# S5 entry and exit and second MLP entry of a hybrid trunk kernel: splits, scalings and sums at other places of the engines' programs

## Chip, cores and metric

The kernel runs on one core of a Trainium2 chip. The metric is the device time of one launch in microseconds; lower is better. Engines are named as in the profile: PE is TensorE, DVE is VectorE, ACT is ScalarE, POOL is GpSimd, and SP is the sequencer that issues most of the DMAs.

## What is computed

The input is 256 frames of 2048 channels in float32, and there are two layers. Layer 0 is an RG-LRU beside sliding-window attention, followed by an MLP. Layer 1, which the change touches, is cut to this:

```
h = rmsnorm(x, mix_norm_o)
y = s5_grouped(h, ...)          # 128 groups: 16 channels in, 64 complex states, scan over frames, 16 out
g = gelu(y) @ w_glu             # 2048 x 4096
val, gate = split(g)
x = x + val * sigmoid(gate)
h = rmsnorm(x, ffn_norm[1])
x = x + square(relu(h @ w_up)) @ w_down      # 2048 x 8192 x 2048
```

## The kernel before, in words

The engines run programs of their own, in order, tied by semaphores. Nearly all of the time is matrix products on TensorE in float32r. Every product is made of a high and a low part of both operands, so a weight goes through three steps. SP loads a unit of 512 KB into one of four buffers `raw`. ScalarE makes the high part `Wh` (line 1162), and VectorE the difference `Wl` (line 1575). SP loads a buffer again only when VectorE has split it. `split(g, s)` is unit s of pair g; four units make a pair. ScalarE's `split` waits for the unit's landing and until TensorE is done with the unit that was in the buffer before.

The norm of the S5 layer: TensorE sums squares (line 1025), ScalarE takes the root, VectorE inverts it and signals `rss_ready` (line 1619, in `inv_root`). The root scales the S5 inputs `us`.

The S5 stage works on 16 chunks c of 128 channels each:

- `s5_input(c)` (line 2402, GpSimd) multiplies the chunk by the inverse root. Six chunks are done ahead of the loop, the others beside it, as `inputs_beside` lists. `input_rows` (line 2382) issues the DMA that brings two chunks of `us` in another order.
- `s5_in(c)` (line 1000, TensorE) multiplies by the input weights. From c = 13 (`V_ALONE`) on it has one result bank instead of two.
- `s5_rotate(c)` (lines 2009 and 2010, VectorE) multiplies by cosine and sine; `s5_turned(c)` (line 2409, GpSimd) takes their difference; `s5_scan(c)` (line 2018 and two multiplications, lines 2023 and 2024, VectorE) runs the recurrence and turns back; `s5_unturned(c)` (line 2415, GpSimd) sums.
- `s5_out(c)` (lines 1013 and 1018, TensorE) multiplies by the output weights; `s5_gelu(c)` (line 1443, ScalarE) follows and signals `s5_ge`.
- SP stores the result (line 619) and loads it in the order of frames, `load_turned` (line 608). It does the latter for chunk c only after the low part of chunk c - 4 is done.
- `s5_high(c)` (line 1448, ScalarE) and `s5_low(c)` (line 2421, GpSimd) make the operand of the GLU and signal `a2_ready`. GpSimd does the low parts of chunks 0 to 7 inside its loop, and those of 8 to 15 after `s5_unturned(15)`.

The order within each engine is written out by hand. SP's program ahead of and in the S5 loop is this; `load_glu` (line 601) loads a GLU unit:

```
for u in range(2 * NU): load_glu(0, u)          # NU = 4
...
for c in range(KC):
    sp.wait_ge(s5_ge, c + 1)                    # then the store of chunk c
    ...                                         # parameter rows of later chunks
    if c >= 1: load_turned(c - 1)
load_turned(KC - 1)
for u in range(2 * NU, 4 * NU): load_glu(0, u)
```

The GLU goes in four blocks j of 16 units. A unit of block 0 has two halves (frames 0 to 127 and 128 to 255) of six products each. From chunk 8 on TensorE does one half (`glu_piece`) per step of the S5 loop, in the order of `GLU_PIECES`, and the remaining units after the last output (`glu_block(0, 4)`, lines 1046 to 1048). Each block ends with a gate, a sum into `xin`, and a transposition back to channels (`turn_back`).

The second MLP's first pair of units needs the operands of GLU block 3 in its last unit: TensorE turns them back beside the second unit, and ScalarE (`operand_back`, line 1501) and VectorE (line 1934) make high and low parts. For the norm ScalarE squares the frames (`frame_squares(3)`, line 1492), VectorE makes two diagonals (line 1949), TensorE sums (`frame_sum`, line 1121, after the first pair), ScalarE loads the root's table and takes the root (lines 1185 and 1187), and VectorE inverts it (`rms`) before it reads the first pair's result.

## Time and profile before

| | us |
|---|---|
| runs shown | 2005.13, 2011.80, 2007.59 |
| their median | 2007.59 |
| the profiled execution: its time | 2006.38 |
| the profiled execution: its span | 2004.6 |

The span is from the first to the last instruction in the profile, 1.8 us less than the execution's own time. In the span TensorE is busy for 1967.2 us, VectorE for 1294.2, ScalarE for 927.6 and GpSimd for 705.8. The S5 stage lies at about 1048 to 1125 us, the GLU from there to about 1290, and the second MLP behind it. A matmul's end is modelled in the profile, and successive ones overlap, so start-to-start distances are the ones to read.

### The profile page before, as it was taken

The numbers are of one execution on the slowest core, as the hardware profiler recorded it, in microseconds if no ns is written. First come the engines' busy times: TensorE is split into PE (matmuls) and PEld (weight loads), VectorE is DVE, ScalarE is ACT, GpSimd is POOL, SyncE is SP. The second block draws the span as 40 slices with busy tenths as digits, with TensorE's granted clock in tenths as the row PEclk, the third lists the DMA queues.
The fourth block names the chain that finished last, engine by engine and source line by source line (L and its number), as shares of the span: only waits on it lengthen the run. The fifth ranks groups of instructions, "written<-read, shape, count | busy, mean of one in ns | idle before, by whom it ended". The sixth has DMA issues, their size and how long they took to land.

```text
span 2004.6 us, 32978 instructions
## 1 busy us (share of the span) xinstructions
PE 1967.2 (98%) x12214; PEld 1682.6 (84%) x12214; DVE 1294.2 (65%) x1428; ACT 927.6 (46%) x1211; POOL 705.8 (35%) x893
## 2 busy tenths in 40 slices
PE   8999999999999999999998999999999999999999
PEld 7778888888888888888887788888888888888887
DVE  6886787765765676567669555576556556655654
ACT  6456654444444444444553544544344434434442
POOL 3483368998777778440239300000000000000000
PEclk9999999999999999999998999999999999999999
DMA  7544568666766676676888566655566566555654
GB/s 224 172 123 130 169 180 225 192 210 214 225 201 221 197 224 205 218 250 204 275 272 298 181 185 179 188 182 192 194 187 191 190 192 186 189 194 184 189 193 164
DMA packets 326549, 400.29 MB, mean 200 GB/s; under 512 B 23328, under 2 KB 267184, under 8 KB 324368
## 3 DMA queue, kind: packets, MB, share of 16 engines
q1 hardware_dynamic: 318992, 371.77, 58.9%
q0 software_dynamic: 5216, 24.52, 4.0%
q8 instruction: 98, 1.61, 0.3%
q10 hardware_dynamic: 2208, 2.11, 0.3%
q14 instruction: 35, 0.29, 0.0%
HBM read 371.87 MB, written 25.17 MB: 198 GB/s over the span
## 4 chain that ended last, share of the span: by engine, by line
PE 89%; DVE 5%; ACT 2%; POOL 2%; issue 1%; DMA 1%; SPq 0%; ACTq 0%; POOLq 0%; DVEq 0%
PE ps L724 38%; PE ps L725 19%; PE ps L691 6%; PE ps L692 6%; PE ps L693 6%; DVE Wl L1575 2%; PE px L1047 1%; PE px L1048 1%; PE px L1046 1%; PE ps L1046 1%; PE ps L1047 1%; PE ps L1048 1%; PE px L944 1%; ACT Wh L1162 1%; POOL us L2402 1%
## 5 line engine op out<-in xcount | busy, mean ns | idle before, releaser
L724 PE MATMUL ps<-A,Wh 128*128 128x512 f32 x3520 | 1239.2, 397 | 4.5 <-issue 2.1
L1575 DVE TENSOR_TENSOR Wl<-raw,Wh 128x1024 fp32r<-128x1024 f32 x660 | 837.8, 1281 | 591.8 <-ACT Wh L1162 589.0
L1162 ACT ACTIVATE Wh<-raw 128x1024 fp32r<-128x1024 f32 x660 | 690.7, 1058 | 738.7 <-PE ps L725 446.5
L725 PE MATMUL ps<-A,Wl 128*128 128x256 f32 x3520 | 981.2, 279 | 0.0
L724 PEld LDWEIGHTS ps<-A,Wh 128*128 128x128 f32 x3520 | 661.1, 188 | 165.0 <-issue 6.9
L725 PEld LDWEIGHTS ps<-A,Wl 128*128 128x128 f32 x3520 | 663.3, 188 | 0.4
L691 PE MATMUL ps<-Wh,A 128*128 128x512 f32 x512 | 199.2, 389 | 0.0
L692 PE MATMUL ps<-Wl,A 128*128 128x512 f32 x512 | 199.2, 389 | 0.0
L693 PE MATMUL ps<-Wh,A 128*128 128x512 f32 x512 | 199.2, 389 | 0.0
L691 PEld LDWEIGHTS ps<-Wh,A 128*128 128x128 f32 x512 | 96.1, 188 | 20.1
L693 PEld LDWEIGHTS ps<-Wh,A 128*128 128x128 f32 x512 | 96.1, 188 | 20.0
L692 PEld LDWEIGHTS ps<-Wl,A 128*128 128x128 f32 x512 | 96.1, 188 | 19.7
L1896 DVE TENSOR_TENSOR A<-cross,A 128x512 f32 (+1 forms) x64 | 47.5, 741 | 57.4 <-ACT A L1533 32.4
L1646 DVE TENSOR_TENSOR cross<-ps,cross 128x512 f32<-128x512 f32 x112 | 76.5, 683 | 6.8 <-ACT cross L1167 6.5
L2118 POOL TENSOR_TENSOR sq<-xT 128x512 f32<-128x512 f32 x15 | 24.4, 1624 | 131.4 <-issue 73.5
L1359 ACT ACTIVATE A<-cross 128x512 fp32r<-128x512 f32 (+1 forms) x32 | 20.2, 632 | 108.5 <-DVE cross L1893 108.5
L1167 ACT ACTIVATE cross<-ps 128x512 f32<-128x512 f32 x114 | 66.2, 581 | 1.1 <-PE ps L677 1.1
L1533 ACT ACTIVATE A<-cross 128x512 f32 (+1 forms) x32 | 20.2, 632 | 97.7 <-DVE cross L1893 97.7
L1046 PE MATMUL ps<-Wh,A 128*128 128x512 f32 x128 | 51.2, 400 | 1.0 <-DVE Wl L1575 1.0
L1046 PE MATMUL px<-Wh,A 128*128 128x512 f32 x128 | 50.1, 392 | 0.0
L1047 PE MATMUL ps<-Wl,A 128*128 128x512 f32 x128 | 49.9, 390 | 0.0
L1048 PE MATMUL ps<-Wh,A 128*128 128x512 f32 x128 | 49.9, 390 | 0.0
(389 smaller groups left out, 1967.8 us busy)
## 6 DMA issues: line engine op xcount, KB each, us to landing
raw<-in_w_up_dram SPq DMA_DIRECT2D x256, 512.0 KB, 3.9
raw<-in_w_down_dram SPq DMA_DIRECT2D x256, 512.0 KB, 3.9
raw<-in_w_glu_dram SPq DMA_DIRECT2D x64, 512.0 KB, 4.0
raw<-in_w_in_e_dram SPq DMA_DIRECT2D x52, 512.0 KB, 3.9
raw<-in_w_out_e_dram SPq DMA_DIRECT2D x32, 512.0 KB, 3.4
s_params<-stg POOLq DMA_DIRECT2D x16, 1024.0 KB, 5.7
slot<-s_params SPq DMA_DIRECT2D x12, 768.0 KB, 6.8
slot<-s_params SPq DMA_DIRECT2D x12, 256.0 KB, 6.4
```

Source lines behind the costliest of these rows:

```text
L691: mm(to, high, wide(Wh, u % NU)[:, c], start=(k == 0), stop=False)
L692: mm(to, high, wide(Wl, u % NU)[:, c], start=False, stop=False)
L693: last = mm(to, low, wide(Wh, u % NU)[:, c], start=False, stop=(k == KC - 1))
L724: mm(ps[:, b + t, :], Wh[:, s, c, cols], A[:, k, :], start=(n == 0), stop=False)
L725: last = mm(ps[:, b + t, 0:L], Wl[:, s, c, cols], A[:, k, 0:L], start=False, stop=(n == KC - 1))
L1046: mm(to, high, wide(Wh, u % NU)[:, c], start=(k == 0), stop=False)
L1047: mm(to, high, wide(Wl, u % NU)[:, c], start=False, stop=False)
L1048: last = mm(to, low, wide(Wh, u % NU)[:, c], start=False, stop=(k == KC - 1))
L1162: fn(Wh[:, s], raw[:, s], ACT.Copy).then_inc(hi_split, 1)
L1167: fn(cross[:, d], banks[:, :, L:2 * L], ACT.Copy).then_inc(crossed, 1)
L1575: tt(Wl[:, s], raw[:, s], Wh[:, s].bitcast(F32), ALU.subtract).then_inc(lo_split, 1)
L1646: tt(cross[:, d] if dest is None else dest, banks[:, :, 0:L], cross[:, d], ALU.add).then_inc(pair_read, 1)
```

## The change

It touches three places.

At the S5 entry VectorE scales chunk 0 itself, right after the inverse root, and signals a semaphore of its own (`us_first`); GpSimd scales chunks 1 and 2 ahead of its loop instead of 0 to 5, then issues the DMA of the last two chunks' rows, which before stood ahead of the root, and does the other scalings in its loop. Of VectorE's two splits ahead of its loop the second (unit 3 of the GLU) goes to step 13 of the loop.

At the S5 exit unit 4 of the GLU is done in halves: one between outputs 14 and 15, one behind output 15. ScalarE does its splits of units 5 and 6 ahead of the gelu of chunk 14, and that of unit 7 ahead of the gelu of chunk 15. SP's load of unit 7 goes from ahead of its loop to step 13, behind `load_turned(12)`.

At the second MLP the diagonals are made beside the first unit, TensorE's sum follows the transposition beside the second unit, the root's table is loaded beside the first split, and root and inversion are done beside the third unit.

The diff, cut to its core:

```diff
@@ constants, line tables @@
-INPUTS_AHEAD = 6
+INPUTS_AHEAD = 3
+        us_first = sem("us_first")
-        GLU_PIECES = ((0, 0), (0, 1), (1, 0), (2, 0), (2, 1), (1, 1), (3, 0), (3, 1))
+        GLU_PIECES = ((0, 0), (0, 1), (1, 0), (2, 0), (2, 1), (1, 1), (3, 0), (3, 1), (4, 0), (4, 1))
-            return {0: (6,), 1: (7, 8), 2: (9,), 3: (10, 11), 4: (12,), 5: (13, 14), 6: (15,)}.get(c, ())
+            return {0: (3, 4), 1: (5,), 2: (6, 7), 3: (8,), 4: (9, 10), 5: (11,)}.get(c, (c + 6,) if c < KC - 6 else ())
@@ sync: loads @@
-            for u in range(2 * NU):
+            for u in range(2 * NU - 1):
                 load_glu(0, u)
...
                 if c >= 1:
                     load_turned(c - 1)
+                if c == V_ALONE:
+                    load_glu(0, 2 * NU - 1)
@@ tensor @@
-                pe.wait_ge(us_ready, c + 1)
+                if c == 0:
+                    pe.wait_ge(us_first, 1)
+                else:
+                    pe.wait_ge(us_ready, c)
...
             s5_out(KC - 2)
+            glu_piece(8)
             s5_out(KC - 1)
-            glu_block(0, 4)
+            glu_piece(9)
+            glu_block(0, 5)
...
+                def last_block(s):
+
+                    if s == 1:
+                        turn_back(3, px)
+                        frame_sum()
...
-                             beside=(lambda s: turn_back(3, px) if s == 1 else None) if q == 0 and j == 0 else None)
-                        if q == 0 and j == 0:
-                            frame_sum()
+                             beside=last_block if q == 0 and j == 0 else None)
@@ scalar @@
             for c in range(KC):
                 if c + 2 < KC:
                     s5_decay(c + 2)
+                if c == KC - 2:
+                    split(P_GLU + 1, 1)
+                    split(P_GLU + 1, 2)
+                if c == KC - 1:
+                    split(P_GLU + 1, 3)
                 s5_gelu(c)
                 if c >= 3:
                     s5_high(c - 3)
-                if c in (10, 14):
-                    split(P_GLU + 1, (c - 10) // 4)
-            s5_high(KC - 3)
-            split(P_GLU + 1, 2)
-            s5_high(KC - 2)
-            split(P_GLU + 1, 3)
-            s5_high(KC - 1)
+                if c == 10:
+                    split(P_GLU + 1, 0)
+            for c in range(KC - 3, KC):
+                s5_high(c)
...
-                    pair(q * 16 + j + g0, (g0 + d) % 2, before=rms if first else None,
-                         beside=last_operand if first else None)
+                    pair(q * 16 + j + g0, (g0 + d) % 2, beside=last_operand if first else None)
...
                     if s == 0:
                         frame_squares(3)
+                        act.preload_act_table(ACT.Sqrt)
                     if s == 1:
                         operand_back(3, px)
+                    if s == 2:
+                        var.wait(act)
+                        root.inc(fn(rs[:, :], nv[:, :], ACT.Sqrt))
@@ vector @@
                     if s == 1:
                         operand_back(3, px)
                     if s == 2:
+                        rms()
+                    if s == 0:
                         dve.wait_ge(xss_ready, 8)
...
-                    up(g0, j, d, q, isinstance(q, int) and q == 0, after=q * 8 + j + (CROSSED + 1),
+                    up(g0, j, d, q, False, after=q * 8 + j + (CROSSED + 1),
...
+            dve.wait_ge(rss_ready, 1)
+            dve.wait_ge(u_loaded[0], 16)
+            tt(us[:, 0], us[:, 0], rss[:, :].unsqueeze(1).to_broadcast([P, TPC, NC4]), ALU.mult).then_inc(us_first, 1)
             split(P_GLU, 2)
-            split(P_GLU, 3)
...
             for c in range(KC):
+                if c == V_ALONE:
+                    split(P_GLU, 3)
@@ gpsimd @@
             input_rows(KC // 2 - 2)
-            input_rows(KC // 2 - 1)
...
             pool.wait_ge(rss_ready, 1)
-            for c in range(INPUTS_AHEAD):
+            for c in range(1, INPUTS_AHEAD):
                 s5_input(c)
+            input_rows(KC // 2 - 1)
```

## Rows read from the trace of the kernel before

**Rows 1.** The page, part 1 (busy us, share of the span) and part 5

```profile
PE 1967.2 (98%) x12214; PEld 1682.6 (84%) x12214; DVE 1294.2 (65%) x1428; ACT 927.6 (46%) x1211; POOL 705.8 (35%) x893
...
L1162 ACT ACTIVATE Wh<-raw 128x1024 fp32r<-128x1024 f32 x660 | 690.7, 1058 | 738.7 <-PE ps L725 446.5
```

**Rows 2.** Waits, all engines, 880 to 1180 us (total, times, longest)

```profile
DVE ab L2009 <- PE px L1000: 2.2, 5, 1.0
```

**Rows 3.** Timeline of VectorE, S5 entry (start us, length us, engine, line)

```profile
1049.63 0.23 DVE L1619 TENSOR_TENSOR rss<-rss,nw 128x64 f32<-128x64 f32 x1
...
1053.68 0.69 DVE L2009 TENSOR_TENSOR ab<-px,slot 128x512 f32<-128x512 f32 x1 [1.03 <-PE px L1000]
...
1059.72 0.68 DVE L2009 TENSOR_TENSOR ab<-px,slot 128x512 f32<-128x512 f32 x1
...
1092.64 0.68 DVE L2009 TENSOR_TENSOR ab<-ps,slot_over_sums 128x512 f32<-128x512 f32 x1
```

**Rows 4.** Timeline of TensorE at the S5 entry (in brackets: idle before)

```profile
1051.68 1.97 PE L1000 MATMUL px<-us,slot 64*64 64x64 f32 x32 [3.96 <-issue]
...
1056.88 1.15 PE L1000 MATMUL ps<-us,slot 64*64 64x64 f32 x32
1061.12 0.48 PE L1013 MATMUL px<-us,slot 64*64 64x64 f32 x4 [3.09 <-POOL pp L2415]
```

**Rows 5.** Timeline of TensorE at the S5 exit

```profile
1117.50 0.33 PE L1013 MATMUL px<-us,slot 64*64 64x64 f32 x4 [1.05 <-POOL pp L2415]
...
1119.04 0.50 PE L1046 MATMUL ps<-Wh,A 128*128 128x512 f32 x1
...
1125.75 0.50 PE L1046 MATMUL ps<-Wh,A 128*128 128x512 f32 x1 [0.96 <-DVE Wl L1575]
```

**Rows 6.** Timelines of TensorE, ScalarE and VectorE, second MLP entry

```profile
1299.87 0.47 PE L724 MATMUL ps<-A,Wh 128*128 128x512 f32 x1 [0.43 <-DVE A L1934]
...
1315.01 0.47 PE L724 MATMUL ps<-A,Wh 128*128 128x512 f32 x1 [0.58 <-issue]
...
1295.84 1.06 ACT L1162 ACTIVATE Wh<-raw 128x1024 fp32r<-128x1024 f32 x1 [0.34 <-PE ps L725]
...
1304.34 1.28 ACT L1185 ACT_TABLE_LOAD   x1
...
1298.07 1.65 DVE L1934 SCALAR_TENSOR_TENSOR A<-px,pcol,A 128x256 fp32r<-128x256 f32 x4
```

**Rows 7.** Timeline of GpSimd, S5 entry; then lines 2402 and 2415 whole

```profile
1050.54 5.45 POOL L2402 TENSOR_TENSOR us<-us,rss 128x256 f32<-128x256 f32 x6
1055.95 1.26 POOL L2409 TENSOR_TENSOR zb<-ab 128x512 f32<-128x512 f32 x1
...
L2402 POOL TENSOR_TENSOR us<-us,rss x16: 716/730/1705, 1050.5 to 1079.4; 128x256 f32<-128x256 f32 x16
...
L2415 POOL TENSOR_TENSOR pp<-pp x16: 1185/1188/2098, 1059.9 to 1115.3; 128x512 f32<-128x512 f32 x16
```

**Rows 8.** Windows, each engine's busy us; last: granted clock, DMA share, GB/s

```profile
1050.00:1052.00 2.00, 0.32 (x6) 0.35 (x8) 2.00 (x2) 1.97 (x4) 1.98 (x3) 0.52 0.36 74
```

**Rows 9.** Timelines of VectorE and ScalarE at the S5 exit

```profile
1115.18 1.22 DVE L1575 TENSOR_TENSOR Wl<-raw,Wh 128x1024 fp32r<-128x1024 f32 x1
...
1119.16 0.38 ACT L1443 ACTIVATE yb<-px 128x256 f32<-128x256 f32 x1 [0.80 <-PE px L1018]
```

**Rows 10.** SP at the exit: its waits, its timeline, line 601's landings

```profile
SPq L607 <- POOL A L2421: 4.1, 1, 4.1
...
1118.33 0.32 SPq L608 DMA_DIRECT2D yt<-s_y_d  x1
...
1121.05 0.43 SPq L619 DMA_DIRECT2D s_y_d<-yb  x1
...
1123.60 24.48 SPq L601 DMA_DIRECT2D raw<-in_w_glu_dram  x13
...
DMA to landing us min/median/max: 3.8/4.8/5.3
```

## The prediction

> **What bounds the kernel now.** I read the page first. TensorE is busy for 98% of the span [rows 1], so any gain or loss has to appear as time in which it waits or runs at the lower clock. I then looked for its waits. Between the two MLPs, in the S5 stage, the waits of VectorE for TensorE are few and short, 2.2 us in 5 times [rows 2]; there VectorE sets the pace. Its first multiplication of a chunk starts at 1059.72 us for chunk 2 and at 1092.64 for chunk 11, nine steps of 3.66 us with no idle time between [rows 3]. So what matters at the entry is when this chain starts, and afterwards when TensorE, which from chunk 8 on also has GLU half units to do, gets through. TensorE waits 3.96 us ahead of the first S5 input and 3.09 us ahead of the first output [rows 4]. At the exit it waits 1.05 us for GpSimd's last sum and 0.96 us for a split [rows 5]. At the second MLP it waits 0.43 and 0.58 us [rows 6]. All times below are on the clock of the profiled execution; where an earlier part has moved everything, I count from the unmoved time and add the shift at the end.
>
> **Entry.** The reciprocal root is finished at 1049.63 + 0.23 = 1049.86 [rows 3]. Before, GpSimd then scaled six chunks in 5.45 us, and only then turned chunk 0 [rows 7]. After, VectorE scales chunk 0. The trace has no such operation of VectorE; for 256 elements it lies between its 0.23 us for 64 and its 0.69 for 512 [rows 3], in proportion at 0.43, and GpSimd's median is 0.73 [rows 7]. I take 0.45, with 0.25 and 0.73 as bounds. TensorE starts at 1050.4 instead of 1051.68. The first input takes 2.0 us until VectorE reads it (1051.68 to 1053.68) [rows 3, 4], so VectorE's read comes at 1052.4 and chunk 1's at 1054.1. One split of 1.23 us instead of two stands in VectorE's way and is over by then. GpSimd is free, turns chunk 0 from 1053.8 to 1055.0, and the first scan starts at 1055.4, after two multiplications of chunk 1. It and two products take the 2.5 us that are left of a step of 3.66 after the two multiplications, so chunk 2's multiplication starts at 1057.85 against 1059.72: 1.9 us gained. GpSimd has three more scalings inside its loop (0.7 us each); per step it has 3.66 us, and a sum (1.19), a turn (1.26) and one or two scalings [rows 7] fill 3.2 to 3.9 of them by their own lengths, as they did before, when VectorE still kept its 3.66; so I cost them at nothing, but for the rival below. The input rows' DMA, moved behind two scalings, falls into GpSimd's idle time before chunk 0's turn. Bounds of the gain: 1.2 us if GpSimd's first scaling goes ahead of VectorE's and holds it for 0.73; 2.5 us if the clock is still full for the first input. It fell to half at about 1050.1, as a granted mean of 0.52 over 1050 to 1052 says [rows 8], so a start at 1050.4 just misses it.
>
> One of GpSimd's scalings took 1.705 us against a median of 0.73; the six ahead of the loop, beside VectorE's splits, took 5.45, a whole microsecond over six medians [rows 7]. The Trainium skill (SBUF — State Buffer, section Who interferes with whom) says that a VectorE instruction with two SBUF inputs and a GpSimd instruction that reads SBUF block each other for a whole instruction. By that rule the outcome here hangs on which of the two scalings goes first, and the entry would gain 1.9 or 1.2; the trace agrees that such a wait occurs.
>
> **Exit, the intended part.** VectorE's split of unit 3 (1.23 us) [rows 9] moves into the loop ahead of chunk 14. It falls partly into VectorE's waits of some 0.4 us (2.2 in 5) [rows 2]; I take 0.4 us of delay for the last chunk, bounds 0 and 1.2. The split of unit 4 starts at 1115.6 instead of 1115.18 and ends at 1116.8. TensorE ends output 14 at 1117.50 - 1.05 = 1116.45 [rows 5], waits until 1116.9, does the first half of unit 4 (1.4 us: two whole units take from 1119.04 to 1125.75 - 0.96 = 1124.79, 2.9 each, the last one's drain of 0.1 included), output 15 (1.5, 1117.50 to 1119.04), and the second half: 1121.2. Units 5, 6 and 7 end at 1129.6. Before, unit 6 started at 1125.75 [rows 5] and unit 8 at 1131.3. So if all splits come in time, 1.7 us are gained. ScalarE's two splits ahead of output 14's gelu fit into its idle time, and cost nothing while that output comes after 1116.3.
>
> **Exit, what is queued behind.** Unit 7's load is moved too, from ahead of the loop to SP's step 13, behind the load of turned chunk 12. That load waits on a count of low parts that only chunk 8's, done by GpSimd after its last sum, completes: SP waited 4.1 us for it and issued at 1118.33 [rows 10]. So unit 7's load, before issued ahead of the whole loop, now comes behind GpSimd's last sum, and ScalarE's split of unit 7 waits for its landing with the last gelu, the last store and the loads of units 8 and on behind it. The chain: GpSimd's last sum, beside a split, took 2.10 us against a median of 1.19 [rows 7]; with the 0.4 us delay and three VectorE splits in a row beside it I put chunk 8's low part 1.1 us later (bounds 0.3 and 1.7), at 1119.4. Unit 7's issue follows at 1119.8, its landing after 3.8 us [rows 10] at 1123.6, ScalarE's split of 1.06 us [rows 1] at 1124.65, the last gelu (0.38) [rows 9] at 1125.05, against a store at 1121.05 before [rows 10]. From that store to the load of unit 8 SP took 2.55 us (1123.60), so now 1127.6. Its landing takes 3.8 to 4.8 us, its splits 1.06 and 1.23: TensorE starts unit 8 between 1133.8 and 1134.8; I take 1134.2, near the low end as the queue is empty. It has then waited 4.6 us, from 1129.6. Against 1131.3 before, 2.9 us are lost in spite of the intended gain.
>
> **The clock.** After the waits of 3.96 and 3.09 us TensorE ran at 1.2 GHz; 1.15 us for the input at 1056.88 against 1.97 for the first [rows 4, 8] show that it came back to 2.4 at about 1057, some 5.4 us after the restart. A wait of 4.6 us is longer than both, so I count 5.4 us at half speed: 2.7 us lost, bounds 0 and 3.
>
> **Second MLP.** Moving the root's table load (1.28 us) [rows 6] ahead of ScalarE's second split fills its 0.34 us of idle time [rows 6] and delays split and last operands by 0.95 us; unit 3, which waits for them (1299.87, 0.43 idle) [rows 6], starts 1.0 us later, the column sum of 0.4 us having moved from behind it to before it. So the second pair starts 0.6 us later. The third pair then needs no wait of 0.58 [rows 6], since root and squares end 2 us sooner. Sum: 0.0, bounds -0.6 and +0.6.
>
> **Sum.** -1.9 + 2.9 + 2.7 + 0.0 = +3.7 us. The profiled execution took 2006.38 us, so 2010.1; the median of the runs lies 1.2 above it, and by the median I say 2011.3. A measurement of this kernel can tell 0.3%, 6 us, from no change.
>
> **Rivals.** First, *TensorE never gets to the wait* (faster side): the load of unit 8 comes soon enough. Then entry and exit give -1.9 - 1.7 = -3.6, 2004.0. It decides at unit 8's issue: by 1129.6 - 0.1 - 1.23 - 1.06 - 3.8 = 1123.4, 4.2 us before my estimate. For it speaks only that loads are normally far ahead; against it the 4.1 us wait of SP and three tasks in series [rows 10]. Chance 0.15. Second, *the clock holds*: wait as forecast, no fall, +1.0, 2008.6. For it speaks that waits of about 1 us left the clock at full [rows 5]; against it both waits of over 3 us. Chance 0.15. Third, *slow landings*: both loads in series take 5.3 instead of 3.8 us [rows 10], and the splits and GpSimd alternate so that chunk 8's low part comes 0.6 later still: +3.6 more, +7.3, 2014.9. Chance 0.12. Fourth, *GpSimd becomes the bound at the entry*: the three scalings now fall beside low parts in steps 7 to 9, each 0.27 us over 3.66, and GpSimd's first scaling goes ahead of VectorE's (0.7): 1.5 of the 1.9 us are given back, +5.2, 2012.8. Against it, TensorE's own load is the longer from chunk 8 on. Chance 0.10. The forecast keeps 0.48.
>
> **How the numbers follow.** 2004.0 to 2014.9 holds forecast, bounds and all but the ends of the outer rivals: I take 2003.8 to 2015.0. Over 6 us slower needs the third rival or several upper bounds of the forecast: 0.15. Over 6 us faster is beyond the first rival: 0.03. Within: 0.82.
>
> **What would show it.** The scaling by VectorE at about 1049.9 and chunk 2's multiplication near 1057.9; unit 7's load issued right behind the load of turned chunk 12, after GpSimd's first low part past the last sum; ScalarE idle some 4 us for that load; the last gelu 3 to 4 us later than output 15; TensorE waiting 4 to 5 us in front of unit 8 with a granted clock near 0.5 behind it; the 0.58 wait at the third pair gone, the one ahead of unit 3 about 1.1. I am wrong if unit 7's load is issued before GpSimd's last sum, or if TensorE has no wait over 2 us after 1125 in the GLU.

## The result, and the profile after

| | before | after |
|---|---|---|
| median of 20 runs, us | 2010.69 (2004.47 to 2014.93) | 2014.93 (2010.12 to 2021.45) |
| ratio, 95% interval | | 1.0026 (1.0015 to 1.0036) |
| the profiled execution: its time, its span | 2006.38, 2004.6 | 2010.12, 2008.3 |

The change makes the kernel slower, by 0.26% or 5.2 us as the ratio of the two sets of runs has it (the medians lie 4.2 apart): the interval excludes no change. The forecast was +3.7 us on the profiled execution, and the two profiled executions lie 3.7 us apart; not all of that is the change's, as follows.

Each trace is one execution, and the code upstream, which is the same in both, ended at another time: the inverse root at 1049.86 us before [rows 3] and at 1050.99 + 0.23 = 1051.22 after. So in this section and in the experiments I count from the end of the root. A few marks are enough (the gate is ScalarE's first instruction on a block's gates, lines 1511 before and 1525 after; it is read to hundredths here, and the recorded expectations have the same mark to a tenth, as 107.1):

| us | before | after |
|---|---|---|
| end of the root, from the span's start | 1049.86 | 1051.22 |
| root to the first multiplication of chunk 2 (entry) | 9.86 | 7.82 |
| root to the first gate of the GLU | 104.35 | 107.04 |
| first gate to the last one of the fourth block | 136.4 | 136.4 |
| from there to the second MLP's first product of 512 frames | 91.1 | 90.7 |
| from there to the end | 622.9 | 622.9 |

2.0 us are gained at the entry and 4.7 lost between the entry and the first gate; the rest of the kernel is as it was but for 0.4 us behind the last gate. The page is too coarse to see it: TensorE's busy time is the same within 1 us [rows 1].

```profile
PE 1966.2 (98%) x12214; PEld 1681.0 (84%) x12214; DVE 1296.6 (65%) x1429; ACT 927.3 (46%) x1211; POOL 702.9 (35%) x892
```

**Entry.** VectorE's timeline after, which answers to [rows 3]:

```profile
1050.99 0.23 DVE L1636 TENSOR_TENSOR rss<-rss,nw 128x64 f32<-128x64 f32 x1
1051.25 0.42 DVE L2021 TENSOR_TENSOR us<-us,rss 128x256 f32<-128x256 f32 x1
1051.59 1.75 DVE L1592 TENSOR_TENSOR Wl<-raw,Wh 128x1024 fp32r<-128x1024 f32 x1
1053.79 0.69 DVE L2030 TENSOR_TENSOR ab<-px,slot 128x512 f32<-128x512 f32 x1 [0.45 <-PE px L1006]
...
1059.04 0.68 DVE L2030 TENSOR_TENSOR ab<-px,slot 128x512 f32<-128x512 f32 x1
```

TensorE's, to [rows 4], with the idle time before in brackets:

```profile
1051.78 1.97 PE L1006 MATMUL px<-us,slot 64*64 64x64 f32 x32 [2.71 <-issue]
1053.51 1.76 PE L1006 MATMUL ps<-us,slot 64*64 64x64 f32 x32
1055.22 1.15 PE L1006 MATMUL px<-us,slot 64*64 64x64 f32 x32
...
1060.43 0.33 PE L1019 MATMUL px<-us,slot 64*64 64x64 f32 x4 [2.12 <-POOL pp L2437]
```

And GpSimd's, to [rows 7]:

```profile
1051.30 2.63 POOL L2424 TENSOR_TENSOR us<-us,rss 128x256 f32<-128x256 f32 x2 [7.73 <-DVE rss L1636]
1053.87 0.92 POOL L2405 DMA_DIRECT2D us<-s_u  x1
```

VectorE scales chunk 0 in 0.42 us right behind the root, TensorE waits 2.71 us where it waited 3.96, and 2.12 ahead of the first output where it waited 3.09. GpSimd's two scalings, issued 0.05 us after VectorE's, take 2.63 us together against a median of 0.73 each [rows 7], and the split beside them 1.75 against 1.22 [rows 9]. They hold one another up, but VectorE's scaling, which counts, is first. The Trainium skill, SBUF — State Buffer, section Who interferes with whom, has it that the order of issue decides who is blocked. The trace agrees, and so do the nine other traces with the entry part: 0.42 or 0.43 us for VectorE's scaling each time. None of the ten has GpSimd's scaling first, so what the reverse order costs is not shown here.

**Exit.** SP's timeline and its wait, to [rows 10]:

```profile
1118.50 0.32 SPq L609 DMA_DIRECT2D yt<-s_y_d  x1
1118.86 1.29 SPq L602 DMA_DIRECT2D raw<-in_w_glu_dram  x1
...
1125.29 0.36 SPq L620 DMA_DIRECT2D s_y_d<-yb  x1
1125.75 1.74 SPq L609 DMA_DIRECT2D yt<-s_y_d  x2
1127.54 10.69 SPq L602 DMA_DIRECT2D raw<-in_w_glu_dram  x8
```

```profile
SPq L608 <- POOL A L2443: 5.4, 1, 5.4
```

ScalarE's timeline, to [rows 9]:

```profile
1115.35 0.38 ACT L1455 ACTIVATE yb<-px 128x256 f32<-128x256 f32 x1 [0.30 <-PE px L1024]
...
1123.94 1.06 ACT L1174 ACTIVATE Wh<-raw 128x1024 fp32r<-128x1024 f32 x1 [7.64 <-DMA raw<-in_w_glu_dram]
1124.90 0.37 ACT L1455 ACTIVATE yb<-px 128x256 f32<-128x256 f32 x1
...
1131.54 1.06 ACT L1174 ACTIVATE Wh<-raw 128x1024 fp32r<-128x1024 f32 x1 [0.47 <-DMA raw<-in_w_glu_dram]
```

TensorE's, to [rows 5]:

```profile
1115.62 0.50 PE L1052 MATMUL ps<-Wh,A 128*128 128x512 f32 x1 [0.32 <-DVE Wl L1592]
...
1117.20 0.33 PE L1019 MATMUL px<-us,slot 64*64 64x64 f32 x4
...
1126.31 0.50 PE L1052 MATMUL ps<-Wh,A 128*128 128x512 f32 x1 [0.47 <-DVE Wl L1592]
...
1133.90 0.80 PE L1052 MATMUL ps<-Wh,A 128*128 128x512 f32 x1 [4.58 <-DVE Wl L1592]
...
1136.63 0.50 PE L1052 MATMUL ps<-Wh,A 128*128 128x512 f32 x1
```

Read from the top: SP stands 5.4 us at the load of turned chunk 12, until GpSimd has done the first low part behind its last sum, and only then (1118.86) issues unit 7's load. ScalarE stands 7.64 us for its landing, with output 15 finished at about 1118.8 and its gelu queued behind the split until 1124.90. The last store (1125.29), the last turned chunks (1125.75) and the load of unit 8 (1127.54) follow, and TensorE waits 4.58 us ahead of unit 8. (Unit 7's load can't stay ahead of the loop: it goes into the buffer of unit 3, whose split by VectorE has moved to step 13.) The intended part worked: the first half of unit 4 stands between outputs 14 and 15, and the wait of 1.05 us for GpSimd's last sum is gone.

The windows of that stretch, with the granted clock third from the end:

```profile
1132.00:1134.00 2.00, 0.10 (x1) 0.10 (x1) 1.25 (x2) 1.65 (x2) 0.00 (x0) 0.86 1.04 405
1134.00:1136.00 2.00, 2.00 (x5) 1.61 (x6) 1.86 (x2) 1.54 (x2) 0.00 (x0) 0.50 0.77 220
1136.00:1138.00 2.00, 2.00 (x8) 1.59 (x8) 1.79 (x2) 0.57 (x1) 0.00 (x0) 0.79 0.78 275
```

From 1133.90 to 1136.63, 2.7 us, TensorE runs at 1.2 GHz.

**Second MLP.** TensorE and then ScalarE, to [rows 6]:

```profile
1300.54 0.71 PE L1129 MATMUL px<-sq,ones 128*128 128x128 f32 x4
...
1304.89 0.47 PE L727 MATMUL ps<-A,Wh 128*128 128x512 f32 x1 [0.83 <-DVE A L1951]
```

```profile
1299.56 1.28 ACT L1552 ACT_TABLE_LOAD   x1
```

The sum now stands ahead of unit 3, and the wait ahead of the third unit pair is gone; the one ahead of unit 3 grew from 0.43 to 0.83 us.

### The profile page after: what moved, and what is told of

The parts are those of the page before. It is cut to its first block, busy times and chain, and to the rows that moved or that the text cites. A ratio compares the mean times of both kernels' runs of the same rounds, so it can differ in the third digit from the quotient of the medians.

```text
span 2008.3 us, 32979 instructions
## 1 busy us (share of the span) xinstructions
PE 1966.2 (98%) x12214; PEld 1681.0 (84%) x12214; DVE 1296.6 (65%) x1429; ACT 927.3 (46%) x1211; POOL 702.9 (35%) x892
## 4 chain that ended last, share of the span: by engine, by line
PE 89%; DVE 6%; ACT 2%; POOL 1%; issue 1%; DMA 1%; SPq 0%; ACTq 0%; DVEq 0%; POOLq 0%
PE ps L727 38%; PE ps L728 19%; PE ps L695 6%; PE ps L696 6%; PE ps L694 6%; DVE Wl L1592 2%; PE px L1053 1%; PE px L1054 1%; PE px L1052 1%; PE ps L1052 1%; PE ps L1054 1%; PE ps L1053 1%; PE px L947 1%; ACT Wh L1174 1%; PE px L916 1%
## 5 line engine op out<-in xcount | busy, mean ns | idle before, releaser
L1663 DVE TENSOR_TENSOR cross<-ps,cross 128x512 f32<-128x512 f32 x112 | 76.3, 682 | 6.7 <-ACT cross L1179 6.5
L1910 DVE SCALAR_TENSOR_TENSOR cross<-cross 128x512 f32<-128x512 f32 x64 | 49.3, 770 | 2.2
```

The source lines that it names most:

```text
L1663: tt(cross[:, d] if dest is None else dest, banks[:, :, 0:L], cross[:, d], ALU.add).then_inc(pair_read, 1)
```

## The experiments

Theory: the whole loss comes from unit 7's load. Placed behind the load of turned chunk 12 it waits for GpSimd's last sum; the last gelu is queued behind its split, unit 8's load behind the last gelu; the clock falls behind the wait. Rivals: the new order of the last half units costs by itself; the entry or the MLP part gives time back; the exit is bound by something else. Each row below is a kernel that was run, with its ratio to the kernel before. Then follow, in us from the end of the root, the issue of the loads of units 7 and 8; TensorE's wait ahead of unit 8; and the way to the first gate, cut in three by VectorE's first multiplications of chunks 2 and 15: entry, loop and exit, which add up to the gate. Each comparison has 30 or 35 runs of the kernel before on the same chip and 11 or 12 of the other, but 6 of e5; the first of the changed kernel has 20 and 20. The columns in us are of one trace each.

| kernel | ratio (95%) | unit 7 | unit 8 | wait | entry | loop | exit | gate |
|---|---|---|---|---|---|---|---|---|
| before | 1 | ahead of the loop | 73.7 | none | 9.86 | 49.11 | 45.38 | 104.35 |
| after, first trace | 1.0026 (1.0015 to 1.0036) | 67.6 | 76.3 | 4.58 | 7.82 | 48.97 | 50.25 | 107.04 |
| e11_after_again | 1.0016 (1.0003 to 1.0029) | 68.2 | 76.5 | 4.60 | 7.95 | 49.42 | 49.90 | 107.27 |
| e5_exit_only | 1.0032 (1.0020 to 1.0044) | 69.0 | 77.4 | 5.17 | 9.26 | 48.93 | 51.73 | 109.92 |
| e3_entry_only | 1.0005 (0.9997 to 1.0014) | ahead | 74.1 | none | 8.86 | 50.65 | 45.09 | 104.60 |
| e4_mlp_only | 1.0003 (0.9994 to 1.0012) | ahead | 74.8 | none | 9.86 | 50.15 | 45.38 | 105.39 |
| e1_load_first | 1.0000 (0.9990 to 1.0009) | 62.5 | 73.4 | 2.29 | 7.69 | 49.71 | 45.88 | 103.28 |
| e2_gelu_first | 1.0010 (0.9999 to 1.0020) | 67.6 | 74.2 | 2.68 | 7.39 | 49.40 | 48.18 | 104.97 |
| e6_loaded_ahead | 1.0010 (1.0000 to 1.0019) | ahead | 75.0 | 1.37 | 8.85 | 50.64 | 44.93 | 104.42 |
| e8_low_in_loop | 0.9995 (0.9985 to 1.0006) | 61.8 | 70.7 | 0.58 | 7.39 | 48.79 | 44.18 | 100.36 |
| e7_loads_early | 0.9988 (0.9977 to 0.9998) | 63.6 | with unit 7 | none | 8.00 | 50.51 | 43.26 | 101.77 |
| e9_both | 0.9983 (0.9970 to 0.9995) | 62.5 | with unit 7 | none | 8.00 | 49.34 | 43.26 | 100.60 |
| e10_both_no_mlp | 0.9983 (0.9972 to 0.9994) | 65.0 | with unit 7 | 0.44 | 7.95 | 51.64 | 44.00 | 103.59 |
| e12_exit_mended | 0.9990 (0.9979 to 1.0000) | 64.9 | with unit 7 | none | 9.25 | 50.54 | 43.31 | 103.10 |

The lines behind the marks: VectorE's chunk 15, TensorE's unit 8 and line 1511 before, then VectorE's chunk 15 and line 1525 after. The timelines have the first gate at 1154.21 and 1158.26.

```profile
1108.83 0.69 DVE L2009 TENSOR_TENSOR ab<-px,slot 128x512 f32<-128x512 f32 x1 [0.32 <-PE px L1000]
1131.36 0.39 PE L1046 MATMUL ps<-Wh,A 128*128 128x512 f32 x1
L1511 ACT ACTIVATE cross<-ps x4: 591/596/600, 1154.2 to 1245.3; 128x512 f32<-128x512 f32 x4
```

```profile
1108.01 0.68 DVE L2030 TENSOR_TENSOR ab<-px,slot 128x512 f32<-128x512 f32 x1
L1525 ACT ACTIVATE cross<-ps x4: 593/596/599, 1158.3 to 1249.4; 128x512 f32<-128x512 f32 x4
```

The exit column is the one to read for the exit: the kernels that leave the exit alone have 45.1 to 45.4 in it. The loop column varies by almost 3 us, and not with the edits: it is 48.9 to 49.4 in both traces of the changed kernel, in the kernel before and in the exit alone, and 50.2 and 50.5 in e4 and e12, which have no entry part. In all traces VectorE waits in that stretch only for TensorE (0 to 2.8 us in all) and never for GpSimd; the last section says what TensorE's part in it is.

### The parts alone

**The exit alone**, on the kernel before: the half units, ScalarE's and VectorE's splits and SP's load as in the change, nothing else.

```diff
-            for u in range(2 * NU):
+            for u in range(2 * NU - 1):
                 load_glu(0, u)
...
                     load_turned(c - 1)
+                if c == V_ALONE:
+                    load_glu(0, 2 * NU - 1)
```

> The kernel before with the exit part of the change alone (two half units of unit 4, the split orders of ScalarE, unit 3's split in VectorE's loop, unit 7's load behind turned chunk 12); entry and second MLP as before. Theory A: the wait ahead of unit 8 is there, 4 to 5 us; root to first gate is 104.3 + 4.8 = 109.1 (108 to 111), +4 to +7 us in all, ratio 1.002 to 1.0035, more than the whole change. Theory B gives the same loss here, but then with GpSimd's last sum as the event the length of the wait follows. Theory C (the loss of the changed kernel lies outside the exit, in the entry's or the MLP's new order): root to first gate stays within 1 us of 104.3.

Measured: 1.0032, as much as the whole change or more; first gate at 109.92, 5.6 us later than before, with an exit 6.3 us longer. Theory A in all its numbers but the wait, which is 0.2 over. TensorE's timeline and the windows behind the wait:

```profile
1136.89 0.80 PE L1048 MATMUL ps<-Wh,A 128*128 128x512 f32 x1 [5.17 <-DVE Wl L1581]
```

```profile
1136.00:1138.00 2.00, 1.11 (x3) 0.92 (x4) 1.87 (x2) 1.71 (x2) 0.00 (x0) 0.50 0.66 224
1138.00:1140.00 2.00, 2.00 (x6) 1.56 (x5) 1.84 (x3) 1.33 (x2) 0.00 (x0) 0.50 0.87 248
1140.00:1142.00 2.00, 2.00 (x6) 1.57 (x5) 0.80 (x1) 0.00 (x0) 0.00 (x0) 0.50 0.79 270
1142.00:1144.00 2.00, 2.00 (x9) 1.59 (x9) 0.43 (x1) 1.06 (x1) 0.00 (x0) 0.91 0.87 295
```

Here TensorE runs at half speed for some 5.5 us behind the wait, twice as long as in the changed kernel's trace. The loss is the exit part's.

**The entry alone**, on the kernel before, with both splits still ahead of VectorE's loop:

```diff
-INPUTS_AHEAD = 6
+INPUTS_AHEAD = 3
...
+            tt(us[:, 0], us[:, 0], rss[:, :].unsqueeze(1).to_broadcast([P, TPC, NC4]), ALU.mult).then_inc(us_first, 1)
             split(P_GLU, 2)
             split(P_GLU, 3)
```

> The kernel before with VectorE's scaling of chunk 0, GpSimd's scalings spread over its loop and the last rows' DMA behind two of them; both splits stay ahead of VectorE's loop, exit and MLP as before. Theory A: chunk 2's first multiplication comes 1.2 to 2.0 us earlier after the root (9.86 us before; 7.9 to 8.7), since the second split ahead of the loop takes back up to 0.8; this gain is kept to the first gate: 102.3 to 103.2 against 104.3, ratio 0.999 to 0.9995. Theory C (GpSimd's scalings beside low parts in steps 6 to 9 take the entry's gain back): first gate at 104 or later.

Measured: chunk 2's multiplication came 8.86 us after the root, where 9.86 stood before: a gain of 1.0, less than the 1.2 that was the least expected. The first gate was no earlier (104.60), which is the sign that was set for theory C. Theory C's mechanism is not there, though: the loop took 1.5 us longer, but VectorE waited in it for TensorE (2.6 us against 1.2 before) and not at all for GpSimd, and TensorE's timeline has waits of 1.97 and 1.44 us that the profile puts down to nothing ("issue"). Such waits stand in kernels without the entry part too. No cost of the entry part shows, and alone its gain is too small for the comparison.

**The MLP part alone**, on the kernel before:

```diff
+                        turn_back(3, px)
+                        frame_sum()
...
                     if s == 0:
                         frame_squares(3)
+                        act.preload_act_table(ACT.Sqrt)
```

> The kernel before with the second MLP's entry alone changed. Theory A: last unit of the first pair starts 1.0 us later, the wait of 0.58 us ahead of the third pair goes; from the last gate to the first token block 90.6 to 91.2 us against 91.1 (90.7 in the changed kernel); ratio 0.9995 to 1.0003. Theory C (part of the loss is here): over 92.

Measured: the third pair's wait gone, unit 3's at 0.83, ratio 1.0003. The stretch from the last gate to the first product of 512 frames took 92.2 us, more than the 90.6 to 91.2 expected and over the 92 that was the sign for theory C. But it took 92.2 or 92.3 in six other traces, with the MLP part (e2, e8, e9, e11) or without (e5, e10), and 90.7 to 91.1 in the rest: two paces that come with the part and without it. At the quicker one it took 90.7 in all four traces with the part (after, e1, e6, e7) and 91.0 or 91.1 in the three without, so the part is worth 0.3 to 0.4 us there.

### What is queued behind the load

**Unit 7's load ahead of turned chunk 12** in SP's step 13:

```diff
+                if c == V_ALONE:
+                    load_glu(0, 2 * NU - 1)
                 if c >= 1:
                     load_turned(c - 1)
-                if c == V_ALONE:
-                    load_glu(0, 2 * NU - 1)
```

> The changed kernel, with one edit: in SP's step 13 the load of unit 7 stands ahead of the load of turned chunk 12 instead of behind it. Theory A (the queue: unit 7's load, the last gelu, the last store and unit 8's load are in series behind GpSimd's first low part after its last sum): the load is issued near 1113 us and lands near 1117, ScalarE's wait of 7.6 us for it goes, TensorE's 4.58 us wait ahead of unit 8 and the half clock behind it go. From the end of the inverse root to the first gate of the GLU (104.3 us before, 107.1 in the changed kernel) it takes 100 to 101.5 us; against the kernel before -3 to -4.5 us, a ratio near 0.998. Theory B (the loss comes from VectorE's splits and GpSimd blocking each other around the last sum, since unit 3's split moved into the loop and units 4 to 6 are split in a row): the stretch stays at 106 to 107, for nothing in that order is altered.

SP's timeline, and TensorE's:

```profile
1113.19 0.51 SPq L602 DMA_DIRECT2D raw<-in_w_glu_dram  x1
1118.61 0.33 SPq L609 DMA_DIRECT2D yt<-s_y_d  x1
...
1124.07 1.97 SPq L602 DMA_DIRECT2D raw<-in_w_glu_dram  x4
```

```profile
1130.97 0.50 PE L1052 MATMUL ps<-Wh,A 128*128 128x512 f32 x1 [2.29 <-DVE Wl L1592]
```

Part of what was expected: the slowdown is gone and the clock stays up, and the exit shrinks from 50.25 to 45.88 by this one move, with VectorE's splits and GpSimd's sums in the order of the changed kernel, so theory B is out. But the wait is only halved, the first gate comes at 103.28 and not at 100 to 101.5, and the ratio is 1.0000 and not near 0.998. There is a **second floor**. Unit 8's load stands in SP's queue behind the last store and the loads of the last turned chunks, which wait for the stores to land. It was issued 73.4 us after the root, as in the kernel before (73.7), and over the kernels that wait for unit 8 TensorE starts it 6.4 to 7.0 us after that issue (133.90 - 127.54 = 6.4 after, 130.97 - 124.07 = 6.9 here, less the 1000). Before, it started 7.8 us after the issue (1131.36 - 1123.60; 81.5 from the root), so there was at most 1.4 us to gain in front of it, however well the outputs went, unless that load came sooner too.

**The gelu ahead of the split**, the load left where the change put it:

```diff
+                s5_gelu(c)
                 if c == KC - 1:
                     split(P_GLU + 1, 3)
-                s5_gelu(c)
```

> The changed kernel with one edit: in ScalarE's program the second split of w_gelu's last unit (which waits for that unit's load) stands behind the gelu of chunk 15 instead of ahead of it. The load itself keeps its place in SP's order. All times counted from the end of the root ahead of S5; in the changed kernel the gelu of chunk 15 started at 73.7 us, unit 8's load was issued at 76.3, TensorE waited 4.6 us ahead of unit 8, ScalarE's first gate came at 107.1. Theory A (the wait comes because the last gelu is queued behind the split, so that the last high part, the last loads of turned chunks and with them unit 8's load are late): the gelu of chunk 15 starts at about 67.5 us, unit 8's load is issued at about 72.5 to 73, TensorE waits 1 to 2.5 us ahead of unit 8, the clock does not fall for more than 2 us, the first gate comes at 102.5 to 103.5, and the ratio to the kernel before is 0.999 to 1.001. Theory B (unit 7's load is itself too late; what is queued behind its split does not matter): TensorE then waits for unit 7's own split instead, unit 8's load and the gate stay where they are, within 1 us, and the ratio stays at 1.002 to 1.004.

Theory A's direction, but short of its numbers in all but the gelu and the ratio: the gelu came at 1119.74 - 1052.09 = 67.7, unit 8's load at 74.2 instead of 76.3 (72.5 to 73 expected), the wait at 2.68 instead of 4.58, the first gate at 104.97 (102.5 to 103.5 expected). SP's waits say what was short by 1.5 us:

```profile
SPq L608 <- POOL A L2443: 5.4, 1, 5.4
...
SPq L609 <- DMA s_y_d<-yb: 2.9, 2, 2.6
```

It stood 5.4 us at turned chunk 12 as in the changed kernel, and then 2.6 for a store to land before it could load that chunk turned; in the kernel before such waits were 0.7 us at most. So the queue behind the split is worth 2 us; that the place of the load is worth the rest is what e1 showed from the other side. The clock fell behind this wait too: the first product of unit 8 took 0.80 us, as in the changed kernel, where [rows 5] have 0.50.

**Unit 7's load and unit 3's split back ahead of the loops**, the new order of the half units kept. The two go together, since unit 7's load needs the buffer that unit 3's split empties:

```diff
-            for u in range(2 * NU - 1):
+            for u in range(2 * NU):
                 load_glu(0, u)
...
             split(P_GLU, 2)
+            split(P_GLU, 3)
```

> The changed kernel with unit 7's load and VectorE's split of unit 3 both put back ahead of the S5 loop, where the kernel before has them; the half unit between the last two outputs, the copies beside the loop, the MLP part and the rest stay. Theory A (the late load of unit 7 is what costs, and TensorE's new order is worth nothing by itself since unit 8's load cannot come earlier): no wait of more than 1 us for unit 7, 2 to 2.5 us of waiting ahead of unit 8, the clock falls for less than 2 us, root to the rotation of chunk 2 at 8.6 to 9.2 us (7.8 in the changed kernel), root to the first gate at 103.5 to 104.6 us, ratio to the kernel before 0.999 to 1.001. Theory B (the new order of the last pieces costs by itself, wherever unit 7 is loaded): root to the first gate at 106.5 us or more and a ratio of 1.002 or more.

Theory A: entry 8.85 us, first gate 104.42, ratio 1.0010; only the wait, 1.37, is shorter than the 2 to 2.5 expected. With unit 8's load at 75.0, TensorE's new order of half units costs nothing in the trace and brings 0.45 us at the exit; the ratio, with an interval from 1.0000 to 1.0019, does not show even that.

### Mending it

**Chunk 8's low part inside GpSimd's loop**, so that SP's load of turned chunk 12 needs not wait for the last sum:

```diff
-                if 6 <= c < KC - 2:
+                if 6 <= c < KC - 1:
...
-            for c in range(KC - 8, KC):
+            for c in range(KC - 7, KC):
```

> The changed kernel with one edit on GpSimd: the low part of chunk 8's operand is made inside the loop, in its 15th step, and not behind the loop's last sum, so that the load of turned chunk 12, ahead of which unit 7's load stands in SP's order, does not have to wait as long. Theory A (unit 7's load is late because SP stands at the load of a turned chunk that waits for GpSimd's last sum): unit 7's load is issued about 5 us earlier, at 62 to 63 us from the end of the root (67.6 in the changed kernel), the gelu of chunk 15 starts at 67 to 69 us (73.7), unit 8's load is issued at 70 to 73 us (76.3), TensorE waits under 2.5 us ahead of unit 8, first gate at 100.5 to 103.3 us (107.1), ratio to the kernel before 0.998 to 1.000. Theory B (GpSimd's parts are only moved, SP's wait passes to another load): unit 7's load within 1.5 us of where it is, first gate at 106 us or later, ratio at 1.002 or more.

SP's timeline and TensorE's:

```profile
1113.45 0.45 SPq L602 DMA_DIRECT2D raw<-in_w_glu_dram  x1
...
1122.39 15.72 SPq L602 DMA_DIRECT2D raw<-in_w_glu_dram  x10
```

```profile
1129.08 0.50 PE L1052 MATMUL ps<-Wh,A 128*128 128x512 f32 x1 [0.58 <-DVE Wl L1592]
```

Both loads come 5.6 to 5.9 us sooner, the wait shrinks from 4.58 to 0.58, and the first gate comes at 100.36, 4.0 us ahead of the kernel before: 2.5 at the entry, 0.3 in the loop and 1.2 at the exit. The entry's 2.5 hold 0.4 to 0.6 us of luck (7.39 against 7.82 and 7.95 in the changed kernel), since this trace did its first S5 input at the full clock. One line of GpSimd's program decides whether this change loses. That it gains with that line the trace says alone: the ratio is 0.9995, with an interval of 0.1% to either side.

**Three loads early**: units 7, 8 and 9 ahead of turned chunk 12, and ScalarE's splits of 8 and 9 between its last high parts.

```diff
+                if c == V_ALONE:
+                    for u in range(2 * NU - 1, 2 * NU + 2):
+                        load_glu(0, u)
                 if c >= 1:
                     load_turned(c - 1)
-                if c == V_ALONE:
-                    load_glu(0, 2 * NU - 1)
             load_turned(KC - 1)
-            for u in range(2 * NU, 4 * NU):
+            for u in range(2 * NU + 2, 4 * NU):
                 load_glu(0, u)
...
-            for c in range(KC - 3, KC):
-                s5_high(c)
+            s5_high(KC - 3)
+            split(P_GLU + 2, 0)
+            s5_high(KC - 2)
+            split(P_GLU + 2, 1)
+            s5_high(KC - 1)
```

> The changed kernel with the loads of w_gelu's units 7, 8 and 9 all issued ahead of the load of turned chunk 12, and ScalarE's splits of units 8 and 9 put between its last high parts and not behind them and the switch of table. Theory A (the exit has two floors: the late load of unit 7 and, once that is gone, unit 8's load, which stands behind the last stores and turned chunks; a gain is there only when both are lifted): unit 8's load lands before 70 us from the end of the root, TensorE waits less than 1 us for any of units 7 to 9, the clock stays at full speed, first gate at 99.5 to 101.5 us (104.3 in the kernel before, 107.1 in the changed one, 103.3 with unit 7's load alone moved), ratio to the kernel before 0.997 to 0.999. Theory B (the last output itself, that is the turned chunk 15, is the bound and not the units): the wait moves to the turned chunks since three weight loads now stand ahead of them, first gate at 103 us or more, ratio 1.000 or more.

No wait ahead of units 7 to 9, clock 1.00 throughout, ratio 0.9988: theory A, though the first gate at 101.77 is 0.3 later than its 99.5 to 101.5. The exit took 43.26 us, 2.1 less than before; the loop had taken 1.4 longer.

**Both repairs**:

> The changed kernel with both repairs of the exit: GpSimd makes the low part of chunk 8 inside the loop, and SP loads w_gelu's units 7, 8 and 9 ahead of turned chunk 12, with ScalarE's splits of units 8 and 9 between its last high parts. Theory A (two floors, both lifted; the remaining 1.4 us that the second repair alone was short of the first comes from the turned chunks that wait behind GpSimd's last sum): no wait of more than 0.5 us for units 7 to 9, SP's load of turned chunk 12 about 5 us after unit 7's load and not 6, root to the first gate at 99.5 to 101 us (100.4 and 101.8 with one repair alone, 104.3 in the kernel before), ratio to the kernel before 0.997 to 0.9985. Theory B (TensorE is busy without a gap in either repair alone, so what is left differs by chance): first gate within 0.5 us of 100.4 and a ratio of 0.9985 to 0.9995.

Its edit is the two diffs above together. First gate at 100.60, ratio 0.9983. The exit took 43.26 us, the same as with the second repair alone (SP issued turned chunk 12 5.1 us after unit 7's load, 5.4 there), and the 1.2 us between the gates of the two stand in the loop column. So theory B's reading is right for the trace: the first repair adds nothing to the second at the exit. The ratio lies in theory A's range, but its interval reaches over theory B's. TensorE has no gap and no fall of the clock where it stood for 4.58 us, 78.1 to 82.7 us after the root, which is 1133.0 to 1137.6 here (windows: the length, TensorE's busy time, and the clock third from the end):

```profile
1132.00:1134.00 2.00, 2.00 (x10) 1.68 (x9) 1.28 (x1) 1.98 (x3) 1.59 (x2) 1.00 1.01 358
1134.00:1136.00 2.00, 2.00 (x10) 1.66 (x9) 0.64 (x1) 1.61 (x3) 0.43 (x1) 1.00 1.04 314
1136.00:1138.00 2.00, 2.00 (x11) 1.65 (x10) 1.78 (x2) 1.77 (x2) 0.00 (x0) 1.00 0.76 255
```

This kernel is faster than the kernel before and than the changed one: 2006.97 us median against 2010.00 and 2012.78 on the same chip.

**Both repairs without the MLP part** (the second MLP's lines of the change undone, of which two):

```diff
-                        frame_sum()
...
-                        act.preload_act_table(ACT.Sqrt)
```

> The kernel with both repairs of the exit, but the entry of the second MLP as in the kernel before. Theory A (the MLP part is worth 0.2 to 0.4 us, less than a comparison can tell): ratio within 0.001 of that of the kernel with both repairs, third gate to first token block at 91 to 92 us or, at the quicker of the two paces of matmuls seen in that stretch, 0.2 to 0.5 us more than 90.7. Theory B (the MLP part costs or gives over 2 us somewhere that the stage marks do not show): the ratio is off by over 0.001.

0.9983 again: the MLP part is worth nothing that the ratio can tell; the stretch behind the last gate took 92.3 us, the slower pace. The first gate is 3 us later than with it, though it comes before any code that differs, and 2.3 of the 3 stand in the loop column. One wait of TensorE without a cause in its timeline is of that size:

```profile
1107.15 0.34 PE L1025 MATMUL px<-pp,slot_over_sums 64*64 64x64 f32 x5 [2.06 <-issue]
```

**Both repairs without entry and MLP part**, that is the kernel before with the exit part and the repairs (here one line of the entry part, which is undone):

```diff
-INPUTS_AHEAD = 3
+INPUTS_AHEAD = 6
```

> The kernel before with the exit part of the change and both repairs, without the entry part and without the MLP part. Theory A (the three parts add up, and the exit is worth a gain only when its loads are mended): no wait of more than 0.5 us for units 7 to 9, root to the first gate at 101.5 to 103 us (the entry's 1.5 to 2 us more than with it), ratio to the kernel before 0.998 to 0.9995. Theory B (what the exit gains hangs on the entry part's order of copies and sums): first gate at 104 us or more, ratio 1.000 or more.

First gate at 103.10, ratio 0.9990 (0.9979 to 1.0000), against 0.9983 with the entry: theory A's signs, at the edge of its numbers. The mended exit took 43.31 us, as with the entry part (43.26): it is worth 2.1 us with or without it. The gate is only 1.2 us earlier than before since the loop took 1.4 longer. The entry took 9.25 here and 8.00 in e9. That these 1.25 us last to the end no ratio shows, as the two intervals overlap.

**The changed kernel again**, for a second trace:

> The changed kernel itself once more, without an edit, for a second trace: the profiled execution of the changed kernel was its quickest and spent 2.7 us at half clock, while its other executions had a lower mean clock. Theory A (most executions lose more to the clock after the 4.6 us wait than that one did): about 5 to 6 us at half clock behind the wait, root to the first gate at 107.5 to 110 us, ratio to the kernel before 1.002 to 1.0035. Theory B (the clock dips for 2.7 us after that wait in any execution, and what differs lies in other stages): 2 to 3 us at half clock, first gate at 106.5 to 107.5 us.

```profile
1133.13 0.80 PE L1052 MATMUL ps<-Wh,A 128*128 128x512 f32 x1 [4.60 <-DVE Wl L1592]
```

Theory B: again a wait of 4.60 us, the clock back by 1136.1, that is 3 us at half speed, first gate at 107.27. My reading that most executions lose twice as much to the clock has one trace for it (the exit alone) and two against. The three slowest of the first twenty runs of the changed kernel (2018.49, 2020.36 and 2021.45) are at a mean clock of 0.993, where most of the others have 0.995 to 0.998, so some executions did lose more to the clock. The twelve runs here do not repeat it, and where they lost it no trace shows.

## Why the prediction was right and wrong

**The last step failed: what counts as no change.** The chain that led up to it held, as the next paragraphs show. I wrote that a measurement of this kernel can tell 0.3%, 6 us, from no change, and gave "within" 0.82. I gave no working for that bound; the three runs that I had lie 0.33% apart. Twenty runs of each kernel resolve 0.1%, and the interval, 1.0015 to 1.0036, lies wholly on the slower side and reaches past the bound. The cases themselves said slower: forecast, slow landings, bound at the entry and the holding clock, together 0.85, were all above zero. I should have asked how fine the comparison would be, not how far three runs lie apart. The same three runs gave the base: their median was 2007.59 where twenty gave 2010.69, and of the 3.6 us between my 2011.3 and the 2014.93 measured 3.1 are that. So it is luck that 2014.93 still lies 0.07 us inside my upper end of 2015.0.

**Entry**: forecast -1.9, measured 7.82 - 9.86 = -2.0. VectorE's scaling took 0.42 us (forecast 0.45), and went ahead of GpSimd's. Three extra scalings in GpSimd's loop did not hold VectorE: from chunk 2 to the end of its last chunk it took as long as before within 0.3 us in both traces, so the fourth rival is out, and the 0.4 us of delay that I gave unit 3's split did not show either. (The loop was up to 2.5 us longer in other traces, but in none of them did VectorE wait in it for GpSimd. The rival's 0.27 us was also low: a low part that runs alone takes 0.85, which no row of mine had, and with it such a step comes to 4.03 us and not 3.93.)

**Exit, intended part**: forecast -1.7 if all splits come in time. No run of the change itself shows it. In e8 the exit took 1.2 us less than before, and 2.1 less in e7, e9 and e12, where the loads of units 8 and 9 had been moved as well. That e8's first gate comes 4.0 us earlier, near the first rival's -3.6, is partly luck, for 2.5 of them are the entry's, and its ratio says -1.0 us (-3.0 to +1.2). The rival's point of decision was nearly right. It asked for unit 8's load by 1123.4, which is 71.6 us after the root once the entry's gain is taken off; the changed kernel's was at 76.3, and e8's at 70.7 still left a wait of 0.58.

**Exit, what is queued behind**: the chain went link by link as forecast. In us from the root, forecast (less the entry's 1.9) and measured: unit 7's load 68.0 and 67.6; the end of the last gelu 73.3 and 74.1; unit 8's load 75.8 and 76.3; TensorE at unit 8 82.4 and 82.7, after a wait of 4.6 and 4.58. Against the kernel before (81.5), and with the entry's gain set aside, that is +3.2 where the sum has +2.9. One link was 1.3 us long, the landing of unit 7 (1123.94 - 1118.86 = 5.1 against 3.8), and shorter ones made up for it.

**The clock** was mis-sized. I took 5.4 us at half speed, from the entry, and 2.7 us lost. From the start of unit 8 to the first gate the kernel before took 1154.21 - 1131.36 = 22.9 us, the changed one 1158.26 - 1133.90 = 24.4 and in its second trace 107.27 - 82.87 = 24.4: 1.5 us lost, with 2.7 and 3.0 us at half speed. Where the exit part ran alone it was 5.5 us. The stretch is not a constant of the chip that can be read once and carried to another wait.

**Second MLP**: forecast 0.0, bounds 0.6 to either side. The marks give -0.4, and the ratio of e4, 1.0003, shows nothing. Unit 3's wait grew by 0.4 where I said about 0.7 (0.43 to 1.1).

**Sum**: in the trace -2.0 + 3.2 + 1.5 = +2.7 at the first gate, against a forecast of +3.7; the ratios of the two comparisons say +5.2 (3.0 to 7.2) and +3.2 us (0.6 to 5.8). The first is more than the +2.3 that the first trace shows to its end, and what the runs beyond it lost is not shown. The 3.7 us between the two profiled executions hold 1.4 us that arose ahead of the change and belong to chance. That one number agrees with another is no proof of the sum.

**What I missed** is the second floor. I saw that unit 8's load came 2.55 us behind the last store, and used it for the loss, but not that in the kernel before it already stood within 1.4 us of holding TensorE up. The 1.7 us of the intended exit could never have come in full without moving unit 8's load as well.

## What to carry to other kernels

When a load or a copy is moved later in a queue, list what that queue waits for ahead of it and what is queued behind the instruction that waits for it; here one load moved behind one wait cost 4.6 us of TensorE, and moving a 0.85 us low part out from behind a sum on another engine gave it all back. Look also for the floor under the one that is lifted: how long before TensorE's start on its unit each load is issued ahead of a change (here 7.8 us where 6.4 to 7.0 is the least) says how much there is to gain. Cut the way to a mark into stretches before calling a difference an edit's: the gates of e7 and e9 are 1.2 us apart and their exits are equal. And ask how fine the comparison is before giving a chance to "no change": twenty runs told 0.1% apart where three had spread over 0.3%.

## What the runs showed of the hardware

The same wait of TensorE does not leave the same clock. The wait ahead of the first S5 input was 2.70 or 2.71 us in every kernel with the entry part; the first input took 1.92 to 1.97 us in six of ten traces, 1.65 or 1.66 in two, and 1.15, the full clock's time, in e2 and e8, where the clock fell only during the second. Those two have the shortest entry, 7.39 us, against 7.69 to 8.00 in the six others with one split ahead. Waits of 1.37 and 2.29 us ahead of unit 8 left the clock at 1.00, waits of 2.68, 4.58, 4.60 and 5.17 had it at half behind them, for 2.7 to 5.5 us.

Executions of the same code differ by more than the parts of this change: the root ended between 1049.9 and 1056.0 us; the stretch behind the GLU took either 90.7 to 91.1 or 92.2 to 92.3 us, and nothing between; and TensorE had single waits of up to 2 us in the S5 loop that no releaser explains. These waits are not scattered. In one trace after another they stand in the same places of TensorE's program: 22 to 26 us after the root ahead of the last nine or ten of an input's 32 products, 29 to 32 and 41 to 44 us after it ahead of the last two of four products of an output, and in e4 and e10 at 56 us among an output's products. Mostly only their lengths differ. Added up they are 0.9 us or less in the kernel before, in both traces of the changed one and in the exit alone, and 5.0 in e10, which has the longest loop; but e8, with 2.7, has the shortest. Where they, the two paces and the spread of the root come from stays open; it wasn't tried. So a difference of two traces counts only between marks that enclose the change, and one of 0.1 to 0.3% has to be told by many runs of each kernel.
